# Neighbourhood attention: where the bias strips are negated and masked on VectorE

## What is computed

```
def neighbourhood_attention(q, k, v, rpb):
    qg = q.reshape(B, rows, GRID_W, C_HEADS, HEAD_DIM) * (HEAD_DIM ** -0.5)
    def row_block(args):
        ...
        bias = rpb[:, dr[None, :, None], dc[:, None, :]]
        s = jnp.einsum('bqhd,brqjhd->bhqrj', q_row, k_nb).astype(jnp.float32)
        s = s + bias.astype(jnp.float32)[None]
        p = jax.nn.softmax(...)
        return jnp.einsum('bhqrj,brqjhd->bqhd', p, v_nb)
```

## Time and profile before

| | us |
|---|---|
| median of 3 runs | 3585.2 |
| lowest and highest | 3576.61, 3587.2 |
| the profiled execution | 3587.32 |
| its span, first to last instruction | 3585.5 |

### The profile page before, as it was taken

How to read it: one execution, slowest core, us unless ns; L and a number is a source line. 1 busy time by engine, 2 the same in 40 slices (tenths; PEclk the granted TensorE clock), 3 DMA queues, 4 the chain that set the end, 5 groups by cost and what they waited for, 6 DMA issues and landing times.

```text
span 3585.5 us, 45480 instructions
## 1 busy us (share of the span) xinstructions
PE 3297.9 (92%) x14378; PEld 2571.1 (72%) x14378; DVE 1603.5 (45%) x2800; ACT 795.7 (22%) x1446; POOL 2019.6 (56%) x838
## 2 busy tenths in 40 slices
PE   3969899998989999889999989999899999989996
PEld 2745688886668888756668867888666678868885
DVE  3214544433346443454334446651543435456633
ACT  1313222101322220125231122210143321122201
POOL 2332477885227778531417766788323247757784
PEclk7968999999999999779979999999789989989998
DMA  4251522322102223110212222233101122212231
GB/s 102 62 97 41 152 92 98 105 99 77 47 24 94 94 101 107 62 36 24 73 51 79 97 70 76 99 102 103 42 30 46 49 76 89 87 63 95 98 106 71
DMA packets 100721, 279.35 MB, mean 78 GB/s; under 512 B 37358, under 2 KB 38126, under 8 KB 100642
## 3 DMA queue, kind: packets, MB, share of 16 engines
q1 hardware_dynamic: 100642, 278.34, 24.7%
HBM read 269.66 MB, written 16.45 MB: 80 GB/s over the span
## 4 chain that ended last, share of the span: by engine, by line
PE 84%; DVE 7%; SPq 2%; DMA 2%; issue 2%; ACT 2%; POOL 1%; DVEq 0%; ACTq 0%; another core or an unknown queue 0%; POOLq 0%
PE PA L445 12%; PE PA L447 11%; PE PA L446 11%; PE PB L445 10%; PE PB L447 9%; PE PB L446 9%; PE S L528 6%; PE O L552 5%; PE T L543 3%; SPq L379 1%; DMA raw<-in_w_diff_v 1%; DMA raw<-in_w_out 1%; DVE acc L1035 1%; POOL wl L427 1%; DVE ml L1350 1%
## 5 line engine op out<-in xcount | busy, mean ns | idle before, releaser
L424 POOL TENSOR_TENSOR wh<-raw,zero 128x1024 fp32r<-128x1024 f32 (+2 forms) x416 | 875.2, 2104 | 1492.4 <-PE PB L447 531.8
L427 POOL TENSOR_TENSOR wl<-raw,wh 128x1024 fp32r<-128x1024 f32 (+2 forms) x416 | 1144.6, 2751 | 32.6
L445 PE MATMUL PA<-hh,wh 128*128 128x512 f32 x1392 | 575.9, 414 | 33.4 <-DVE hl L1029 15.0
L446 PE MATMUL PA<-hl,wh 128*128 128x512 f32 x1392 | 556.0, 399 | 0.0
L447 PE MATMUL PA<-hh,wl 128*128 128x512 f32 x1392 | 555.4, 399 | 0.0
L445 PEld LDWEIGHTS PA<-hh,wh 128*128 128x128 f32 x1392 | 268.8, 193 | 174.6 <-issue 93.2
L445 PE MATMUL PB<-hh,wh 128*128 128x512 f32 x896 | 367.4, 410 | 0.0
L447 PE MATMUL PB<-hh,wl 128*128 128x512 f32 x896 | 354.5, 396 | 0.0
L446 PE MATMUL PB<-hl,wh 128*128 128x512 f32 x896 | 354.3, 395 | 0.0
L447 PEld LDWEIGHTS PA<-hh,wl 128*128 128x128 f32 x1392 | 269.7, 194 | 58.8
L446 PEld LDWEIGHTS PA<-hl,wh 128*128 128x128 f32 x1392 | 270.5, 194 | 52.3 <-issue 1.3
(11 more groups left out here) (244 smaller groups left out, 4991.1 us busy)
## 6 DMA issues: line engine op xcount, KB each, us to landing
raw<-in_w_up SPq DMA_DIRECT2D x176, 512.0 KB, 3.2
raw<-in_w_down SPq DMA_DIRECT2D x64, 768.0 KB, 4.3
raw<-in_w_merge SPq DMA_DIRECT2D x48, 768.0 KB, 4.3
raw<-in_w_out SPq DMA_DIRECT2D x32, 512.0 KB, 3.3
raw<-in_w_na_qk SPq DMA_DIRECT2D x16, 512.0 KB, 3.3
strips_na<-in_rpb SPq DMA_DIRECT2D x1, 7620.0 KB, 31.8
strip<-strips_na SPq DMA_DIRECT2D x32, 224.0 KB, 3.8
strip<-strips_rel SPq DMA_DIRECT2D x48, 128.0 KB, 2.6
```

The lines of the kernel that those rows point to most:

```text
L424: nc.gpsimd.tensor_tensor(wh[s][:, 0:width], raw[s][:, 0:width], zero[:, :].to_broadcast([P, width]), ALU.add).then_inc(w_head, 1)
L427: nc.gpsimd.tensor_tensor(wl[s][:, 0:width], raw[s][:, 0:width], wh[s][:, 0:width].bitcast(F), ALU.subtract).then_inc(w_split, 1)
L445: mm(dst, h_, rh, start=first, stop=False)
L446: mm(dst, h_, rl, start=False, stop=False)
```

## The change

The masking becomes a function, `mask_strip(head, at)`, called from other places, for neighbourhood attention alone. `strip[0]` of the next group is masked at turn 9 of the group before it, behind `take_q` and the `y_tok` of unit 5. `strip[0]` of group 0 is masked ahead of the loop, before `take_q` and `take_k`. `strip[1]` is masked at turn 2, before the biased pass of unit 2. The count of the chain moves by one accordingly. The arithmetic is the same, and so is the number of instructions: eight maskings a layer.

```diff
@@ units, VectorE @@
-                        if strip_at is not None and qt == 0:
+                        if strip_at is not None and qt == 0 and kind != "na":
                             dve.wait_ge(strip_in[head], strip_at)
-                            if kind == "na":
-                                st = strip[head][:, :].rearrange("p (j k) -> p j k", j=14)
-                                link(STT(out=st, in0=st, scalar=-1.0,
-                                         in1=namask[:, :].rearrange("p (j k) -> p j k", j=1).to_broadcast([P, 14, 64]),
-                                         op0=ALU.mult, op1=ALU.add))
+                        if kind == "na" and t == 2:
+                            mask_strip(1, strip_at)
...
                             if t == n:
                                 take_q(ahead)
+                            if t == n + 1 and kind == "na":
+                                mask_strip(0, strip_at + 32)
...
+            def mask_strip(head, at):
+
+                dve.wait_ge(strip_in[head], at)
+                st = strip[head][:, :].rearrange("p (j k) -> p j k", j=14)
+                link(STT(out=st, in0=st, scalar=-1.0,
+                         in1=namask[:, :].rearrange("p (j k) -> p j k", j=1).to_broadcast([P, 14, 64]),
+                         op0=ALU.mult, op1=ALU.add))
...
+                masked = 1 if kind == "na" else 0
+
                 def group(i, ahead):
-                    chain_at(b["d"] + i * per)
+                    chain_at(b["d"] + masked + i * per)
...
-                    done(per)
-
+                    done(per if ahead else per - masked)
+
+                if masked:
+                    chain_at(b["d"])
+                    mask_strip(0, 32 * b["st"] + 32)
                 dve.wait_ge(s_ready, b["u"] + 1)
                 take_q(b); take_k(b)
```

## The result

The changed kernel takes 3588.1 us (median of 20 runs, 3575.45 to 3599.26), the kernel before 3577.6 us (median of 20, 3568.07 to 3591.29). The ratio is 1.0029, with an interval of 1.0015 to 1.0042: slower by about 10 us. Two later comparisons, on two chips, gave 1.0016 (0.9994 to 1.0037) and 1.0004 (0.9987 to 1.0021). So the change brings nothing, and costs between nothing and 0.4%. Its profiled execution took 3579.6 us, 8.5 us less than its median, and that of before (3587.3 us) lay 9.8 us above its own. The two profiles must therefore be compared by stretch, not by their length.

What follows compares the result with a forecast made beforehand. The prediction took the last groups' stall behind strip 0's masking, and the 1.2 GHz after it, as the bound. Gain 34.6 less 5.2 (wait) and 3.8 (clock) in group 0 gave 25.6 us: 3561 us, range 3549 to 3590.

Steps and rivals of the forecast that it cites:

- What bounded the kernel: Last groups of both layers: masking of strip 0 stalls TensorE about 4 us, then 1.2 GHz instead of 2.4 GHz.
- Groups 1 and 2, nothing: Groups 1 and 2, both layers: maskings were hidden and stay hidden, 0 us for 4 groups.
- Hidden, by 0.6 us: Last groups: third biased pass, behind strip 1's masking, ends at 1847.2; TensorE needs it for its fifth score product at 1847.8.
- 6.4 us to the fifth score product: Axial group: time from first to fifth score product, used to place the last group's fifth at 1847.8.
- The term of 34.6 us: Last groups: 21.5 us each instead of 40.1 and 37.5, gain 18.6 + 16.0 us if the clock stays at 2.4 GHz.
- Rival (E): Last groups: strip 1's masking at the third unit stalls TensorE as long as strip 0's did; change not effective; chance 0.03.
- (C): Both last groups fall in clock anyway: 6 - 9 = -3, 3588 us, no change to be told; chance 0.15.
- (B): One of the two last groups falls in clock anyway at the seam of the groups: gain 11, 3574 us; chance 0.30.
- Group 0, 9.0 us of loss: Group 0, both layers: masking waits for strip 0 ahead of take_q and take_k, 5.2 us; falls of clock, 3.8 us.
- The sum: Whole kernel: 34.6 - 5.2 - 3.8 = 25.6 us gained, 3561 us.
- The range: Whole kernel: 3549 (both last groups keep the clock, short waits in group 0) to 3590 us (past both falling).
- The chances: Whole kernel: faster by more than about 0.3% (11 us) 0.60, within it 0.32, slower by more 0.08.

Runs made afterwards that it cites:

- the last experiment but the repeats: Changed kernel with group 0's strips fetched before its weights and masked before take_q, next groups' strips masked at turns 9 and 10: 3554.55 us, ratio to before 0.9918.
- the four kernels without that wait: Changed kernel with no masking (3554.95 us), copy before exponential in turn three (3567.53), strip 1 masked two turns later (3562.12), or all strips fetched and masked early (3554.55).
- the kernels with the wait for the copy: The changed kernel (3588.1 us), and it with group 0's masking behind take_k (3578.52 us) or group 0's strips fetched ahead of its weights (3579.87 us).

## Why the prediction was wrong

**What bounded the kernel: right.** The last groups at 1.2 GHz behind a stall were where the time was to be had. The bound, without any masking, is 3555 us, and the kernel with all maskings early reaches it.

**Groups 1 and 2, nothing: right.** 32.9 and 32.7 us, and the maskings at 1.09 us. The 1.2 us less in the table is the fall in group 2 of layer 0, which came in three of the four profiles of before and in none of the changed kernel. It came without any masking too, so it is no price of the masking.

**Last groups, "Hidden, by 0.6 us": the step that failed.** Its times were good. The masking of strip 1 was to end 5.0 us behind the first score product and the third pass 5.9; they ended 5.1 and 6.0 behind it (1838.66 and 1839.61, less 1833.58). It did wait for the split that was running, and it did not run beside the next, as the prediction has it: that one, begun at 1837.66 while the masking held on until 1838.66, took 3.60 us where the same instruction took 2.75 at 1831.44, so it was the split that waited. This is what an exclusive lock gives, as the Trainium skill has it (SBUF — State Buffer, "SBUF: two separate sides"), and the trace agrees once more. What failed is the sentence behind it: that TensorE needs this pass for its fifth score product. TensorE comes to the V product of unit 0 first. The V product needs the copy, the copy stands on ScalarE behind the exponential of unit 2, and that needs the pass. I asked who waits for the late instruction, and not who is queued behind the one that waits. In the axial group no exponential is late there, so its 6.4 us to the fifth score product could not show this need. The undisturbed V product comes 5.3 us behind the first score product, here it came 7.4 behind. The term of 34.6 us measured 77.8 - 66.5 = 11.3 us in the table. Where the wait is absent (the last experiment but the repeats) the last groups take 42.4 us, 35.4 less than before: the size was right, the condition was not.

**Rival (E) is nearest to what happened, and I had priced it out.** It spoke of a stall of TensorE by the masking of strip 1, wanted a split of 3.4 us started just before, and said the times spoke against it. There was such a split (1834.27, 3.44 us), begun 2 us before the masking, and the stall was half as long as that of strip 0 (2.0 for 4.0 us). (E) had 0.03, and its time was that of (C), 3588 us. That 3588.1 was measured is luck: (C) meant 3 us more than a kernel before of 3585.2 us, the median of three runs, and over 20 runs that kernel took 3577.6. Both last groups fell, as (C) has it, though not by themselves at the seam. (B) and (C) as a mechanism, a fall without a cause in the change, are refuted for the last groups by the four kernels without that wait: the clock stayed at 1.00 in all eight of them.

**Group 0, 9.0 us of loss: right in kind, near in sum by two errors that cancel.** By the table 3.4 us more on the way to it and 7.1 us within it, both layers together, 10.5 in all. The forecast had 5.2 for the wait, too much, and 3.8 for the clock, too little. The masking won the race with the split in layer 0 too (1.09 us), so the wait was at its lower bound; the clock's share was at its upper bound, two falls' worth a layer.

**The sum.** 11.3 - 10.5 leaves about 1 us, for 25.6 expected. By the stage alone the change is nothing; by the runs it is up to 0.4% slower. That last piece, the whole-program time beside the stage, I can't place.

**The range** (3549 to 3590) held 3588, but only as it was reckoned from 3585.2 us; from 3577.6 us it would have ended at 3582. The chances did not hold: 0.60 was put on faster, since a rival with the same end as (C) was held to be nearly excluded by 0.6 us of slack that belonged to another consumer.

## What to carry to other kernels

When an instruction is moved, follow its delay through every in-order queue that it enters: not only to the engine that reads its result, but to whatever stands behind that reader, and to the consumers of that. The start of a group, where the first units run through without a rhythm yet, was here a bad place for an extra 1 us; two turns later the same instruction with the same wait was free. And fetch an operand before you move its first use ahead, or the queue waits for the DMA instead.

## What the hardware showed that I had not expected

**A short idle was enough, and the way back was long.** In the last groups of the kernels with the wait for the copy, an idle of TensorE of 1.6 to 2.6 us, from 5.4 us behind the start, was followed by the fall to 1.2 GHz in eleven of twelve cases; the twelfth, with 1.7 us, kept 2.4 GHz. In the last groups of the kernels without it, where no idle was over 0.7 us, there was no fall in eight. The idle alone does not decide it: in front of group 0 of the kernel before, 1.02 us were followed by no fall, and group 2 fell without an idle over 0.4 us. What tells these cases apart stays open. What follows the fall in a last group is units of 4.6 us for 2.5, and the level mostly stays low to near the end of the group, though TensorE is busy throughout (32.95 of 35.5 us above). In group 0, where projection steps run beside the units, an idle of 2.74 us brought the clock down for 6.8 us only, and idles of 2.2 to 2.9 us for 3 to 10 us in the other profiles.

**The clock's falls make the spread.** In the 20 runs of the changed kernel the shortest, 3575.45 us, had the highest mean granted clock (0.928) and the longest, 3599.26 us, the lowest (0.922). Executions with the same code in group 2 of layer 1's axial attention differed by 3.8 us there, and the same last group took 23.0 or 35.8 us in the two layers of one execution. A single profile of a kernel like this can be 10 us off its median, as both were here.
